# Two MLPs on one Trainium2 core: the down projections of six of eight groups by Strassen's scheme

## What is computed

```python
def squared_relu_mlp(h, w_up, w_down):
    return jnp.square(jax.nn.relu(h @ w_up)) @ w_down
...
h = rms_norm(x, norm_g[i, 2])
x = x + rms_norm(squared_relu_mlp(h, mlp_w_up[i], mlp_w_down[i]), norm_g[i, 3])
```

## Time and profile before

| what | value |
|---|---|
| median of 3 runs | 2551.72 us |
| profiled execution (span) | 2548.7 us |
| TensorE busy | 2494.2 us, 98% |
| VectorE busy | 918.6 us, 36% |
| ScalarE busy | 836.6 us, 33% |
| GpSimd busy | 542.8 us, 21% |
| one group in the loop | 96.0 us (576 matmuls) and about 0.2 us for the branch |
| mean granted TensorE clock | 0.992 |

### The profile page before, as it was taken

One profiled execution on the slowest core, in us unless ns is written; L12 is line 12 of the kernel. 1 busy time (PEld: TensorE's weight loads), 2 busy tenths in 40 slices (PEclk: granted clock), 3 DMA queues, 4 the chain that ended last, 5 costly groups with the idle time before them and its releaser, 6 DMA issues.

```text
span 2548.7 us, 41743 instructions
## 1 busy us (share of the span) xinstructions
PE 2494.2 (98%) x17518; PEld 2362.4 (93%) x17518; DVE 918.6 (36%) x1813; ACT 836.6 (33%) x1658; POOL 542.8 (21%) x304
## 2 busy tenths in 40 slices
PE   8999999999999999999999999999999999999998
PEld 8888887799999999999999877699999999999997
DVE  6555445427221221222238344507322222222226
ACT  5554545446111121121136455627220120121112
POOL 0101011134121121121126110115211212212213
PEclk9999999999999999999999999999999999999999
DMA  3101101124111111111115100114111111111114
GB/s 110 46 21 43 35 24 41 34 86 135 50 42 41 49 41 41 43 47 41 53 34 162 55 26 18 30 34 157 63 43 42 42 48 41 41 49 41 41 60 130
DMA packets 62720, 138.98 MB, mean 55 GB/s; under 512 B 8544, under 2 KB 39520, under 8 KB 62592
## 3 DMA queue, kind: packets, MB, share of 16 engines
q1 hardware_dynamic: 54720, 130.51, 16.0%
q10 hardware_dynamic: 7808, 6.56, 0.9%
q0 software_dynamic: 64, 0.10, 0.0%
HBM read 117.74 MB, written 19.40 MB: 54 GB/s over the span
## 4 chain that ended last, share of the span: by engine, by line
PE 88%; DVE 5%; ACT 3%; issue 2%; DMA 0%; ACTq 0%; SPq 0%; POOL 0%; DVEq 0%; POOLq 0%
PE banks L223 53%; PE banks L203 21%; PE banks L1942 4%; PE banks L2077 1%; PE banks L2096 1%; DVE y L650 1%; DVE norm_acc_x L610 1%; PE banks L1452 1%; PE banks L1433 1%; PE banks L1420 1%; PE banks L1460 1%; PE banks L2086 1%; ACT banks L522 1%; DVE norm_acc L599 1%; PE banks L2061 0%
## 5 line engine op out<-in xcount | busy, mean ns | idle before, releaser
L166 POOL TENSOR_TENSOR w_lo<-w_raw,w_hi 128x1024 fp32r<-128x1024 f32 x164 | 404.4, 2470 | 1835.9 <-ACT w_hi L159 1835.9
L203 PE MATMUL banks<-h_hi,w_hi 128*128 128x384 f32 (+1 forms) x1224 | 423.3, 346 | 4.4 <-DVE h_lo L2507 1.8
L203 PE MATMUL banks<-h_lo,w_hi 128*128 128x384 f32 (+1 forms) x1224 | 404.6, 331 | 0.0
L203 PE MATMUL banks<-h_hi,w_lo 128*128 128x384 f32 (+1 forms) x1224 | 404.3, 330 | 0.0
L159 ACT CAST w_hi<-w_raw 128x1024 fp32r<-128x1024 f32 x180 | 187.1, 1046 | 464.9 <-DMA w_raw<-in_units 464.8
L223 PE MATMUL banks<-h_hi,w_hi 128*128 128x384 f32 (+1 forms) x1368 | 301.8, 329 | 0.0
L223 PE MATMUL banks<-h_lo,w_hi 128*128 128x384 f32 (+1 forms) x1368 | 301.3, 328 | 0.0
L223 PE MATMUL banks<-h_hi,w_lo 128*128 128x384 f32 (+1 forms) x1368 | 301.3, 328 | 0.0
L223 PE MATMUL banks<-mlp_a_hi,w_hi 128*128 128x384 f32 (+1 forms) x1344 | 297.6, 330 | 1.5 <-issue 1.3
L223 PE MATMUL banks<-mlp_a_lo,w_hi 128*128 128x384 f32 (+1 forms) x1344 | 296.1, 328 | 0.0
L223 PE MATMUL banks<-mlp_a_hi,w_lo 128*128 128x384 f32 (+1 forms) x1344 | 296.0, 328 | 0.0
(11 more groups left out here) (205 smaller groups left out, 3183.0 us busy)
## 6 DMA issues: line engine op xcount, KB each, us to landing
w_raw<-in_units SPq DMA_DIRECT2D x180, 512.0 KB, 3.5
x_scratch<-y SPq DMA_DIRECT2D x48, 192.0 KB, 2.8
norm_x<-x_scratch SPq DMA_DIRECT2D x28, 192.0 KB, 3.2
x_scratch<-y SPq DMA_DIRECT2D x24, 160.0 KB, 1.9
norm_x<-x_scratch SPq DMA_DIRECT2D x20, 160.0 KB, 3.0
y<-in_x SPq DMA_DIRECT2D x16, 192.0 KB, 5.2
out_y<-y SPq DMA_DIRECT2D x16, 192.0 KB, 3.3
norm_x<-in_x SPq DMA_DIRECT2D x12, 192.0 KB, 3.3
```

The costliest lines, as they stand in the source:

```text
L166: c.nc.gpsimd.tensor_tensor(c.w_lo[:, s], c.w_raw[:, s], c.w_hi[:, s].bitcast(F32), ALU.subtract).then_inc(self.ready, 1)
L203: mm = chip.nc.tensor.matmul(out, w, x, start=(first and n == 0), stop=(last and n == 2))
```

## The change

In groups 1 to 6 of each MLP the down projection is no longer computed tile by tile. The group's 4 hidden tiles are 2 pairs along the contraction (kappa = 0, 1; tiles 2 kappa and 2 kappa + 1), the 1088 columns are 2 halves of 544, and the 8 output tiles are 4 pairs (p; tiles p and p + 4). With the hidden pair as A11, A21 (first tile, first and second half of the columns) and A12, A22 (second tile), each pair of output tiles is a 2 x 2 block product, which is made with seven products of quarter operands (the Strassen-Winograd form):

- four sums of activations for each kappa, on VectorE (`add`): S3 = A21 - A11, S1 = A21 + A22, S2 = S1 - A11, S4 = S2 - A12; and high and low parts of A11, S3, A12, S1, S2, S4 and A22 (7 casts on ScalarE, 7 subtractions on VectorE, 544 columns each)
- four blocks of weight differences for each output pair, on VectorE (`mix`, 3 instructions), written into the neighbouring slot, with their own high and low parts. So a pair occupies two of the four slots, and pair p + 1 uses the other two; pair 0 and 2 use slots 0 and 1, pair 1 and 3 slots 2 and 3
- seven products for each output pair, of 2 kappa x 3 passes x 2 banks = 12 matmuls of 272 columns. After each product VectorE adds its two banks to one quadrant of `y` (`take_product`, 544 columns). Three products (2, 5, 6) go on accumulating in banks that have been read once
- `y` is kept in another basis during the loop; `change_basis` (2 instructions on 2176 columns each) turns it before and after.

TensorE's order in the first pair begins with the halves that need only the early hidden tiles (`FIRST`). Both sets move (banks 0 to 2 and 5 to 7). The sums' buffers lie in part in the memory of the norm, so ScalarE's loads of x for the last wave wait for the last product's read. The semaphores of the two MLPs are shared and counted through. In the first group, raw hidden tiles have a buffer each, and one wait on VectorE goes.

The core of the diff:

```diff
+    def mix(self, dve, u0, p, g):
+        s, n = 2 * (p % 2), 3 * self.pair_number(u0, p, g)
+        nc, raw, to = self.chip.nc, self.chip.w_raw[:, s], self.chip.w_raw[:, s + 1]
+        of = lambda x, i: x[:, i * QUARTER:(i + 1) * QUARTER]
+        dve.wait_ge(self.raw_in[s], 16 * self.pair_raw_count(u0, p, g))
+        two = lambda x: x.rearrange("p (j n) -> p j n", j=2)
+        nc.vector.tensor_tensor(two(to[:, 0:2 * QUARTER]), of(raw, 0)[:, None, :].to_broadcast([P, 2, QUARTER]),
+                                two(raw[:, QUARTER:3 * QUARTER]), ALU.subtract).then_inc(self.mixed, 1)
+        dve.wait_ge(self.mixed, n + 1)
+        nc.vector.tensor_tensor(of(to, 2), of(raw, 2), of(to, 0), ALU.subtract).then_inc(self.mixed, 1)
+        dve.wait_ge(self.mixed, n + 2)
+        nc.vector.tensor_tensor(of(to, 3), of(to, 2), of(raw, 3), ALU.subtract).then_inc(self.mixed, 1)
+
+    def high_pair(self, act, u0, p, g):
+        s, nc, c = 2 * (p % 2), self.chip.nc, self.chip
+        act.wait_ge(self.raw_in[s], 16 * self.pair_raw_count(u0, p, g))
+        nc.scalar.copy(c.w_hi[:, s, QUARTER:UNIT], c.w_raw[:, s, QUARTER:UNIT]).then_inc(self.pair_hi, 1)
+        act.wait_ge(self.mixed, 3 * self.pair_number(u0, p, g) + 3)
+        nc.scalar.copy(c.w_hi[:, s + 1], c.w_raw[:, s + 1]).then_inc(self.pair_hi, 1)
+
+    def low_pair(self, pool, u0, p, g):
+        s, n, c = 2 * (p % 2), 2 * self.pair_number(u0, p, g), self.chip
+        pool.wait_ge(self.mixed, 3 * self.pair_number(u0, p, g) + 3)
+        for i, at in enumerate((slice(QUARTER, UNIT), slice(0, UNIT))):
+            pool.wait_ge(self.pair_hi, n + i + 1)
+            c.nc.gpsimd.tensor_tensor(c.w_lo[:, s + i, at], c.w_raw[:, s + i, at], c.w_hi[:, s + i, at].bitcast(F32),
+                                      ALU.subtract).then_inc(self.pair_ready, 1)
...
+        def product(p, i, kappa):
...
+            for n, (w, x) in enumerate(((w_hi, x_hi), (w_hi, x_lo), (w_lo, x_hi))):
+                for c in range(2):
+                    mm = nc.tensor.matmul(chip.banks[:, bank + c, 0:half], w, x[:, c * half:(c + 1) * half],
...
+        def slot_free(g, p, i):
+
+            added = self.READS * g + (self.adds + self.N_PROD * p)
+            if i in (0, 1, 3):
+                if p == 0:
+                    pe.wait_ge(self.up_taken, FF_TILES * g + (self.ups + (3 if i < 2 else 4)))
+                else:
+                    pe.wait_ge(self.prod_added, added + {0: 3, 1: 6, 3: 7}[i] - self.N_PROD)
+            elif i in (2, 5, 6):
+                pe.wait_ge(self.prod_added, added + {2: 1, 5: 2, 6: 4}[i])
...
+        FIRST = [(0, 0), (0, 1), (1, 0), (1, 1), (3, 0), (4, 0), (2, 0), (2, 1), (3, 1), (4, 1), (5, 0), (5, 1), (6, 0), (6, 1)]
+        OTHERS = [(i, kappa) for i in range(self.N_PROD) for kappa in range(2)]
...
+        with act.Fori(PAIRED.start, PAIRED.stop) as g:
+            for i in (2, 3):
+                ws.high_up(act, u0, i, g)
+            for kappa in range(2):
+                square(g, 2 * kappa, self.t_raw[:])
+                for part in (self.A11, self.S3):
+                    high(g, part, kappa)
+                square(g, 2 * kappa + 1, self.a_raw[:, 2 * kappa + 1])
+                for part in (self.A12, self.S1, self.S2, self.S4, self.A22):
+                    high(g, part, kappa)
+                if kappa == 0:
+                    ws.high_pair(act, u0, 0, g)
+            for p in range(1, PAIRS):
+                ws.high_pair(act, u0, p, g)
+            for i in range(2):
+                ws.high_up(act, u0, i, g + 1)
...
+        with dve.Fori(PAIRED.start, PAIRED.stop) as g:
+            for kappa in range(2):
+                take_up(g, 2 * kappa, self.t_raw[:])
+                add(g, kappa, self.S3)
+                low(g, kappa, self.A11)
+                low(g, kappa, self.S3)
+                take_up(g, 2 * kappa + 1, self.a_raw[:, 2 * kappa + 1])
+                if kappa:
+                    take_product(g, 0, 0)
+                for part in (self.S1, self.S2, self.S4):
+                    add(g, kappa, part)
+                for part in (self.A12, self.S1, self.S2):
+                    low(g, kappa, part)
+                if kappa:
+                    ws.mix(dve, u0, 1, g)
+                    take_product(g, 0, 1)
+                for part in (self.S4, self.A22):
+                    low(g, kappa, part)
+                if kappa == 0:
+                    ws.mix(dve, u0, 0, g)
+            for p in range(PAIRS):
+                for i in range(2 if p == 0 else 0, self.N_PROD):
+                    if i == 2 and 0 < p < PAIRS - 1:
+                        ws.mix(dve, u0, p + 1, g)
+                    take_product(g, p, i)
```

More of the change, by code:

```diff
@@ L216, in dense_set @@
     order = [(n, b) for n in range(3) for b in range(NB)]
[L217 to L218 removed]
     for i, (n, b) in enumerate(order):
         w, x = passes[n]
[L221 to L223 removed]
+        mm = chip.nc.tensor.matmul(chip.banks[:, bank0 + b, 0:WIDTH[b]], w, x[:, k, COLS[b]],
                                    start=(k == 0 and n == 0), stop=(k == n_k - 1 and n == 2))
@@ new lines, in part, with slot_banks @@
+    def part(self, part, kappa, of_tiles, of_sums):
+        first, second = slice(0, HALF_T), slice(HALF_T, T)
+        if part in (self.S1, self.S2, self.S4):
+            return of_sums[:, 3 * kappa + (self.S1, self.S2, self.S4).index(part)]
+        tile, half = {self.A11: (0, first), self.S3: (0, second), self.A12: (1, first), self.A22: (1, second)}[part]
+        return of_tiles[:, 2 * kappa + tile, half]
+    def slot_banks(self, slot):
+        at = self.SLOT_BANKS[slot]
+        return self.chip.banks[:, at:at + 2, 0:HALF_T // 2]
@@ L1012, in down, with up @@
                     ws.finish()
-        down(0)
-        with pe.Fori(1, FF_GROUPS - 1) as g:
+        def up(g):
+            for j in range(FF_TILES):
+                ws.wait_up(pe, u0, j, g)
+                if j < 2:
+                    pe.wait_ge(self.prod_added, self.READS * g + (self.adds + j - 1))
+                else:
+                    pe.wait_ge(self.up_taken, FF_TILES * g + (self.ups + j - 1))
+                for k in range(KT):
+                    mm = dense_set(chip, self.SET_BANKS[j % 2], k, KT, k * P, j, chip.h_hi, chip.h_lo)
+                mm.then_inc(self.up_full, 1)
+                ws.finish()
@@ L1016, in tensor @@
+        first_down()
+        with pe.Fori(PAIRED.start, PAIRED.stop) as g:
             up(g)
-            down(g)
+            paired_down(g)
         last = FF_GROUPS - 1
@@ L1150, in vector, with add @@
-        for m in range(KT):
-            take_down(0, m, True)
-        with dve.Fori(1, FF_GROUPS - 1) as g:
-            for j in range(FF_TILES):
-                take_up(g, j)
-                low(g, j)
-            for m in range(KT):
-                take_down(g, m)
+        def add(g, kappa, part):
+            a11, a21 = self.t_raw[:, 0:HALF_T], self.t_raw[:, HALF_T:T]
+            of = lambda x: self.part(x, kappa, self.a_raw, self.s_raw)
+            left, right, op = {self.S3: (a21, a11, ALU.subtract), self.S1: (a21, of(self.A22), ALU.add),
+                               self.S2: (of(self.S1), a11, ALU.subtract),
+                               self.S4: (of(self.S2), of(self.A12), ALU.subtract)}[part]
+            before = self.SUMS * g + (self.sums + 4 * kappa)
+            if part == self.S3:
+                dve.wait_ge(self.squared, FF_TILES * g + (self.ups + 2 * kappa + 1))
+            elif part == self.S1:
+                dve.wait_ge(self.squared, FF_TILES * g + (self.ups + 2 * kappa + 2))
+            else:
+                dve.wait_ge(self.summed, before + (2 if part == self.S2 else 3))
+            nc.vector.tensor_tensor(of(part), left, right, op).then_inc(self.summed, 1)
@@ new lines, in take_down, with change_basis @@
+        def take_down(m):
+            dve.wait_ge(self.down_full, self.downs + m + 1)
+            for y, bank in in_two(chip.y[:, m], chip.banks, self.SET_BANKS[m % 2]):
+                op = nc.vector.tensor_copy(y, bank)
+            op.then_inc(self.y_added if m < KT - 2 else self.prod_added, 1)
+        def change_basis():
+            upper, lower = slice(KT // 2, KT), slice(0, KT // 2)
+            first, second = slice(0, HALF_T), slice(HALF_T, T)
+            for m, cols in ((upper, first), (lower, second)):
+                y = chip.y[:, m, cols]
+                nc.vector.tensor_tensor(y, chip.y[:, upper, second], y, ALU.subtract).then_inc(self.turned, 1)
@@ L2207, in start_gate @@
             act.wait_ge(self.gate_full, 1)
-            for out, bank in in_two(self.b[:, 0], chip.banks, 0, self.GATE_BANK):
+            for out, bank in in_two(self.b[:, 0], chip.banks, self.GATE_BANK):
                 op = nc.scalar.activation(out, bank, ACT.Identity, bias=self.gate_b[:])
@@ L2783, in laid_out @@
             mlp_units += [k_units(x) for x in np.split(up[:, f], FF_TILES, 1)]
```

(9 more changed lines are left out.)

359 lines of the change are left out of this document (232 added, 127 removed).

## The result

The changed kernel takes 2585.24 us, the median of 4 runs (2582.56 to 2587.02), against 2551.99 us for the kernel before (4 runs, 2551.47 to 2554.25): a ratio of 1.0129, 95% interval [1.0117, 1.0140]. The profiled execution spans 2582.3 us, 33.6 more than the one of before. The forecast was slower by 16.8; its sign held and its size was half.

A forecast was written before the change was run, and what follows sets the result against it. TensorE, busy 98% of the span, bounds the kernel. Gain, stalls and clock sum to 12 x (-6.0 + 6.1 + 1.3) = +16.8 us on 2548.7; with 3.0 from span to median, 2568.5 us, range 2522 to 2588.

The forecast's parts named there:

- The gain on TensorE: Down projection: 336 matmuls of 0.125 us replace 288 matmuls taking 48.0 us; gain 6.0 us for a group.
- VectorE's order of events: Timeline from T, TensorE's start of a group's first product: VectorE's sums, mix, reads and low parts, to T+14.96 us.
- The port: Low parts of S4 and A22 held while GpSimd works on pair 1's weights: some 1.9 and 2.9 us, not 0.72.
- The prediction's 0.8 us for the page's word: If the port is held for whole instructions, first-pair operations come about 0.8 us later per group; time 9 us longer.
- The faster rival in which VectorE keeps its turn: VectorE keeps the port from S4's to A22's low part; stalls 3.8 us, 2525 us, up to 2540; chance 0.17.
- no holding at all: GpSimd never holds VectorE's low parts at the port; stalls 2.8 us a group, -38 us, 2513 us; chance 0.10.
- The stalls: TensorE waits four times for VectorE in a group's first pair: 6.1 us in all, against 6.0 us gained.
- the clock stays up: TensorE's clock does not fall in the loop and the stalls stand; +1.2 us, 2553 us; chance 0.13.
- The clock: Around TensorE's 3.35 us stall: 3.4 us at the lower clock, 2.7 of them at 45% loss; 1.3 us a group.
- twice 3.4: Upper bound of TensorE's clock loss for a group: twice 3.4 us at 0.45, 3.1 us.
- the clock stays low for twice as long: TensorE's clock doubly long low, or a held operation delays pair 1; stalls 6.6, clock 2.4, 2588 us and above; chance 0.08.
- Edits at nothing: Changes of basis, first-half sums, product reads and mixes of later pairs, load issue and waits: no time added.

The follow-up runs named there:

- e1: Changed kernel with one more wait: GpSimd starts on pair 1's weights only when VectorE has made A22's low part; 2512.75 us, ratio 0.9839 to before.
- e4: Changed kernel with GpSimd's second operation for pair 1 cut from 1024 to 512 columns (those low weights not the reference's); 2563.74 us, ratio 1.0042 to before.
- e2: Changed kernel with 45 unread matmuls of 240 columns per group filling TensorE's four pauses (some sums come out changed); 2552.52 us, ratio 1.0002 to before.
- e5: Changed kernel with VectorE's and TensorE's orders changed in a group's first pair, no wait added; 2504.63 us, ratio 0.9819 to before.
- e6: As e2, without the 28 filler matmuls of the last pause; 2585.52 us, ratio 1.0135 to before.
- e3: Changed kernel with VectorE reading product 1 before, not after, the mix of pair 1's weights; 2551.14 us, ratio 0.9994 to before.

## Why the prediction was right, and where it was off

**The gain on TensorE** held. 336 matmuls in a down part at 0.1248 us, where 0.125 was taken; 6.07 us gained over 48.0, 6.0 predicted. Over the 48.21 that the down part really took it is 6.28; the prediction left the loop's 0.2 us out of both kernels. The 115.8 ns that the Trainium skill ("TensorE: Matmul & The Clock Gate", Back-to-back issue gap) gives for 272 columns is not borne out by the profile after either; the page gives that formula for a matmul by itself, a condition that the prediction left out.

**VectorE's order of events** held to a tenth of a microsecond. S4's sum ended at T + 4.97 (4.97), the mix of pair 1 at 8.40 (8.36), the read of product 1 at 9.04 (9.00), the low part of S4 at 10.98 (10.86), the one of A22 at 13.78 (13.70). (2,1) started at T + 5.67 (5.74), (5,0) at 9.17 (9.14), (5,1) at 11.03 (11.0), (6,0) at 15.30 (15.1). The reads of products 2 and 3 started 0.75 us apart, not 0.63: that spacing of rows 5 was taken for operations that wait for nothing, and the reads didn't keep it (2.99 us for four). It is 0.1 us of the 0.2 at the end.

**The port** was as the earlier trace rows had it: held low parts of 2.02 and 2.88 us against some 1.9 and 2.9, GpSimd in between the two queued operations (its own two take 4.62 us, and 4.19 in e1, where VectorE is out of the way). e1 and e4 show it from both sides. The Trainium skill ("SBUF — State Buffer", Who interferes with whom) names just this pair, a VectorE instruction with two SBUF inputs against a GpSimd instruction that reads SBUF, and the traces agree: the product reads, with one input in PSUM, were never held. Its "for the whole instruction" is not quite what they show: A22 needs 0.72 us and ended at 844.27, so it ran as if from 843.55, and GpSimd's second operation ended at 843.69, 0.14 later. As 0.14 us is also the part of a VectorE operation that doesn't grow with its columns (worked out from the earlier trace rows), the traces don't tell whether the port was free early or that part doesn't need it. The prediction's 0.8 us for the page's word is too large: three handovers of 0.14 us are 0.42, or 5 us in all and not 9. The faster rival in which VectorE keeps its turn did not come about in this order. e1 goes further than it, since there both of GpSimd's operations stay clear: its stalls are 3.0, not 3.8, and its 2512.75 us are those of the rival "no holding at all" (2.8 and 2513).

**The stalls** sum to 6.43 us, against 6.1. So the step "stalls eat the gain" was right: without the clock, the change would be worth nothing, and e2 measured that (1.0002). This is what the rival "the clock stays up" had put at 2553.

**The clock** is the term that was mis-sized. The text took one stretch of 3.4 us at the lower level for a group, 2.7 us of it worked at 45% loss: 1.3 us. The level and the loss were right: PEclk 0.50, 0.226 us for a matmul instead of 0.125 (45% of the time lost). So was the pause that matters: with the last one short or filled (e1, e2, e5) the clock didn't fall. What failed is the length. It is 6.8 us in seven groups, so that 5.1 us are worked and 2.3 lost; four groups have 10.2 us, which cost nearly the same, and only the first stayed at 3.4. The cost is 2.38 us, between the 1.3 taken and the bound of 3.1 that stood in the text as "twice 3.4".

The trace of before had shown this length. The prediction gives the window behind the second pause of the earlier trace rows (1635 to 1639, PEclk 0.56) but not the one that follows:

```profile
1639.00:1643.00 4.00, 4.00 (x35) 2.90 (x34) 2.01 (x5) 2.30 (x6) 0.00 (x0) 0.59 0.43 135
```

By the prediction's own way of counting that is 0.44/0.5 x 4 + 0.41/0.5 x 4 = 6.8 us at the lower level behind a pause of 1.27 us. With 6.8 us and 45% of the 5.1 us worked, the clock term is 2.3, the sum 12 x (-6.0 + 6.1 + 2.3) = +28.8, and the forecast 2580.5. e6 shows that the three pauses ahead don't matter for the price. What makes a stretch 6.8 us and not 3.4 is not shown: behind e3's pause of 3.01 us nine groups had 3.4, behind e4's shorter one of 2.47 us five had 6.8.

So what came about is in the main the prediction's slowest rival, "the clock stays low for twice as long" (2.4 us for the clock), to which it gave 0.08; its stalls of 6.6 us were more than the 6.43 measured, and its time was "2588 and above". The spans differ by 33.6 us where 16.8 were forecast: 13 come from the clock (12 x 1.1), 4 from the stalls (12 x 0.33), -1 from the matmuls. Two things that the prediction did not have nearly cancel, and that they do is luck: the loop's 0.2 us of before (-2.6) and the stretch between the MLPs (+3.2).

**Edits at nothing** held: no wait behind pair 0 shows in the view of waits, none ends with a transfer, and the changes of basis are 8 operations of 2.42 us, unseen by TensorE. That SyncE's and ScalarE's queues cost nothing is what the absence of such waits shows.
